# A delta rule stage that starts each chunk with the queries, and wide products beside a router's narrow ones

## The reference, cut to what matters

```python
# gated delta rule, one chunk (8 heads; the kernel's chunks have 128 tokens, four in all)
v_new = u_c - w_c @ state
out   = q_c @ state + qk_c @ v_new
state = state * gl_c + k_c.T @ v_new        # read by the next chunk only
# router
g_idx = top_1(softmax(t @ w_grp)); e_idx = top_2(softmax(in_group(t @ w_rt)))
# after the experts: two gathered rows per token are weighted and added,
# then a norm (with a layer norm ahead of it after the first mixture)
h = h + w1 * y[row1] + w2 * y[row2]
```

## Time and profile before

| | |
|---|---|
| median of 3 runs (range) | 2215.73 us (2214.52 to 2217.94) |
| the profiled execution's own time | 2216.83 us |
| its span, from first to last instruction | 2215.1 us |
| around the span | 1.7 us |
| mean granted TensorE clock in the span | 0.969 |

### The profile page before, as it was taken

How to read it: one execution, slowest core, us unless ns; L and a number is a source line. 1 busy time by engine, 2 the same in 40 slices (tenths; PEclk the granted TensorE clock), 3 DMA queues, 4 the chain that set the end, 5 groups by cost and what they waited for, 6 DMA issues and landing times. The chain is left out here.

```text
span 2215.1 us, 21061 instructions
## 1 busy us (share of the span) xinstructions
PE 2118.0 (96%) x8072; PEld 1209.1 (55%) x8072; DVE 907.8 (41%) x1686; ACT 509.3 (23%) x1116; POOL 140.0 (6%) x210
## 2 busy tenths in 40 slices
PE   8999999999999999999799999999998989999995
PEld 4444445488874445444345478454445568654442
DVE  2435446345453125113444666242234467433223
ACT  1111111034341001111331146110004446311000
POOL 1000000001001000100200000000001000001003
PEclk9999999999999998999899999989998999989997
DMA  5334575410022114899636920239993220046996
GB/s 178 91 85 124 156 248 204 145 28 1 2 95 73 71 67 160 301 390 380 240 117 215 336 74 1 69 117 373 387 385 118 81 77 1 3 152 234 371 367 241
DMA packets 206470, 374.25 MB, mean 169 GB/s; under 512 B 22952, under 2 KB 124568, under 8 KB 206112
## 3 DMA queue, kind: packets, MB, share of 16 engines
q1 hardware_dynamic: 87568, 174.13, 24.0%
q10 hardware_dynamic: 105696, 157.30, 20.0%
q0 software_dynamic: 13104, 41.43, 5.1%
HBM read 335.60 MB, written 43.52 MB: 171 GB/s over the span
## 5 line engine op out<-in xcount | busy, mean ns | idle before, releaser
L1543 PE MATMUL bank<-ring,work 128*128 128x512 f32 x768 | 338.4, 593 | 7.5 <-DVE work L1559 3.8
L1543 PEld LDWEIGHTS bank<-ring,work 128*128 128x128 f32 x768 | 142.1, 190 | 170.4 <-issue 165.7
L1554 PE MATMUL bank<-ring_halves,work 128*128 128x512 f32 x384 | 173.0, 593 | 4.0 <-DVE work L1568 4.0
L414 PE MATMUL bank<-featT,ring 128*128 128x512 f32 x384 | 170.8, 598 | 4.6 <-DMA ring<-in_w_in 4.6
L2266 PE MATMUL bank<-ring,featT 128*128 128x512 f32 x384 | 170.7, 606 | 4.2 <-ACT featT L1946 2.6
L1283 PE MATMUL bank<-ring,work 128*128 128x512 f32 x384 | 168.9, 600 | 2.9 <-PEq L2043 1.9
L1565 DVE TENSOR_TENSOR work<-work,bank 128x256 f32<-128x256 f32 x48 | 20.2, 421 | 291.4 <-ACT work L1562 291.4
L2266 PEld LDWEIGHTS bank<-ring,featT 128*128 128x128 f32 x384 | 74.3, 195 | 96.5 <-issue 94.8
L1283 PEld LDWEIGHTS bank<-ring,work 128*128 128x128 f32 x384 | 73.2, 193 | 92.7 <-issue 92.7
L414 PEld LDWEIGHTS bank<-featT,ring 128*128 128x128 f32 x384 | 72.0, 192 | 86.8 <-issue 82.1
L513 PE MATMUL bank<-ring,featT 128*128 128x512 f32 x256 | 110.4, 593 | 0.9 <-PEq L396 0.9
(11 more groups left out here) (427 smaller groups left out, 2900.5 us busy)
## 6 DMA issues: line engine op xcount, KB each, us to landing
ring<-in_w_in SPq DMA_DIRECT2D x16, 2048.0 KB, 13.7
ring<-in_moe_w_gate ACTq DMA_DIRECT2D x28, 1024.0 KB, 9.2
ring<-in_moe_w_up ACTq DMA_DIRECT2D x28, 1024.0 KB, 11.7
ring_halves<-in_moe_w_down ACTq DMA_DIRECT2D x28, 1024.0 KB, 11.3
ring_halves<-in_w_ada SPq DMA_DIRECT2D x48, 512.0 KB, 6.3
y_rows<-work ACTq DMA_DIRECT2D x48, 512.0 KB, 10.8
ring<-in_expert_w_gate ACTq DMA_DIRECT2D x14, 1024.0 KB, 10.3
ring<-in_expert_w_up ACTq DMA_DIRECT2D x14, 1024.0 KB, 13.1
```

Source lines behind the costliest of these rows:

```text
L414: last = nc.tensor.matmul(bank[b % 4][:, :], w[:, k, (b % 4) * P:(b % 4 + 1) * P], featT[:, k, :], start=(k == 0), stop=(k == KD - 1))
L1543: last = nc.tensor.matmul(bank[2 + par][:, :], xgT[par][:, k, :], w_gu[par][:, k, :], start=(k == 0), stop=(k == KD - 1))
L1554: last = nc.tensor.matmul(bank[5 + h][:, :], hT[par][:, k, :], w_dn[par][:, k, span(h)], start=(k == 0), stop=(k == KF - 1))
```

## The change

The change has three parts. In the delta stage each chunk starts with `qT`; ACT copies it ahead of `g`, `e`. The eight `z` products of a chunk stand in four places (`Z_AT`): two at the chunk's start, four behind `kT` (six in the first chunk), one behind the last level, one behind `vn`. The banks of `o` and `s` change so that `sums` wait for `("o", 1)` and only `kT` for `("s", 1)`; DVE does both `oq`, both `sg`, both `o`, both `s`; the last chunk has no state update. In the routers `keep_clock(1)` stands between the logits, `turn(3)` comes before `logits(2)`, `ranks` are followed by two instead of one, `slots` by four instead of five. In the combines DVE's and ACT's copies come ahead of statistics and of the next root, the second `add` of tile 1 comes behind the copies in `cb_b`, and `keep_clock` products are added around the first turn.

```diff
-        pe_n = (["sums", "qT", "kT", "z"] + [("kk", u) for u in units] + ...
+        pe_n = (["qT", "sums", "kT"] + [("kk", u) for u in units] + ...
-        ac_n = (["g", "e", ("qT", 0), ("qT", 1), "rest", "decay", "z"] + ...
+        ac_n = ([("qT", 0), ("qT", 1), "g", "e", "rest", "decay"] + ...
...
-        QS_BANK, O_BANK, S_BANK, Z_BANK = (5, 6), (4, 0), (1, 2), 7
+        Z_AT = (2, 6, 7)
+        QS_BANK, O_BANK, S_BANK, Z_BANK = (5, 6), (0, 1), (5, 6), 7
...
                     if c:
                         AC.wait(pe, "z", c - 1)
-                        z_products(c, 0, KD // 2)
-                        DV.wait(pe, ("s", 1), c - 1)
+                        z_products(c, 0, Z_AT[0])
+                    (transposes of the queries, "qT")
+                    if c:
+                        DV.wait(pe, ("o", 1), c - 1)
                     (running sums, "sums")
-                    (transposes of the queries, "qT")
+                    if c:
+                        DV.wait(pe, ("s", 1), c - 1)
                     (transposes of the keys, "kT")
-                    PE.done(z_products(c, KD // 2 if c else 0, KD), "z")
+                    z_products(c, Z_AT[0] if c else 0, Z_AT[1])
...
+                    z_products(c, Z_AT[1], Z_AT[2])
                     DV.wait(pe, ("add", NL - 1, units[-1]), c)
...
+                    PE.done(z_products(c, Z_AT[2], KD), "z")
                     AC.wait(pe, ("vn", 1), c)
...
-                    for h in halves:
+                    for h in halves if c < T - 1 else ():
+                        DV.wait(pe, ("oq", h), c)
                         (state update, ("s", h))
...
                     logits(0)
+                    keep_clock(1)
                     logits(1)
+                    if gain is None:
+                        keep_clock(1)
+                    turn(3)
+                    keep_clock(1)
                     logits(2)
-                    turn(3)
                     PE.done(logits(3), "logits")
-                    DV.wait(pe, ("x", T - 1))
                     keep_clock(4)
...
-                    keep_clock(1)
+                    keep_clock(2)
...
-                    keep_clock(5)
+                    keep_clock(4)
...
+            def keep_clock(self, pe, n):
+                pe.wait_ge(AC.sem, AC.value(("row", 3)))
+                for _ in range(n):
+                    nc.tensor.matmul(bank[2][:, :], ident[:, :], level_mask[:, 0:4, :].rearrange("p a n -> p (a n)"), start=True, stop=True)
...
                 cb_a.sums(pe)
+                cb_a.keep_clock(pe, 2)
...
                 cb_a.turn(pe, 0, turn_banks)
+                cb_a.keep_clock(pe, 1)
                 job(0)
...
                 cb_a.norm(act, 0)
+                cb_a.keep_act(act, 0, turn_banks[0])
                 cb_a.ln_root(act, 1)
-                cb_a.keep_act(act, 0, turn_banks[0])
...
                 cb_a.add(dve, 1)
                 cb_a.keep_dve(dve, 0, turn_banks[1])
+                cb_a.statistics(dve, 1)
                 cb_a.layer_norm(dve, 1)
...
                 cb_b.turn(pe, 0, turn_banks)
+                cb_b.keep_clock(pe, 2)
                 latent(0, 0)
...
-                cb_b.add(dve, 1)
+                cb_b.add(dve, 1, of=(0,))
                 cb_b.keep_dve(dve, 0, turn_banks[1])
+                cb_b.add(dve, 1, of=(1,))
                 cb_b.add(dve, 2)
```

More of the change, by code:

```diff
@@ L872, in _ @@
                 for c in range(T):
+                    PE.wait(act, "qT", c)
+                    for h in halves:
+                        AC.done(nc.scalar.activation(qT[:, hs(h), :], b4(3 + h), ACT.Copy), ("qT", h))
                     PE.wait(act, "sums", c)
@@ L876, in _ @@
                     AC.done(nc.scalar.activation(sc[:, 464:480], sc[:, 448:464], ACT.Exp), "e")
-                    PE.wait(act, "qT", c)
-                    for h in halves:
-                        AC.done(nc.scalar.activation(qT[:, hs(h), :], b4(3 + h), ACT.Copy), ("qT", h))
                     DV.wait(act, "rest", c)
@@ L901, in _ @@
                         AC.done(nc.scalar.activation(vnew[:, hs(h), :], b4(2 + h), ACT.Copy), ("vn", h))
+                    PE.wait(act, "z", c)
+                    AC.done(nc.scalar.activation(q_tok[:, c, 0:BANK], bank[Z_BANK][:, :], ACT.Copy), "z")
             @block.vector
@@ L1869, in add_names, with stat_names @@
             def add_names(self, t):
-                return [("add", t, 0), ("add", t, 1)] + ([("half", t, 0), ("half", t, 1), ("mean", t)] if self.ln else [])
+                return [("add", t, 0), ("add", t, 1)]
+            def stat_names(self, t):
+                return [("half", t, 0), ("half", t, 1), ("mean", t)]
             def ln_names(self, t):
@@ L1969, in add @@
                     dve.wait_ge(AC.sem, AC.value(("alpha", t)))
-                for i, w in enumerate((self.rows.w1, self.rows.w2)):
+                for i in of:
+                    w = (self.rows.w1, self.rows.w2)[i]
                     if i:
@@ L1974, in add, with statistics @@
                     DV.done(nc.vector.scalar_tensor_tensor(out=x, in0=self.rows.y_in[2 * t + i], scalar=w[:, t:t + 1], in1=x, op0=ALU.mult, op1=ALU.add), ("add", t, i))
-                if self.ln:
-                    dve.wait_ge(DV.sem, DV.value(("add", t, 1)))
-                    for h in range(2):
-                        DV.done(nc.vector.bn_stats(self.stats[t][:, 6 * h:6 * h + 6], resid[:, t, span(h)]), ("half", t, h))
-                    dve.wait_ge(DV.sem, DV.value(("half", t, 1)))
-                    DV.done(nc.vector.bn_aggr(self.mv[:, t, :], self.stats[t].rearrange("p (a b) -> p a b", a=2)), ("mean", t))
+            def statistics(self, dve, t):
+                dve.wait_ge(DV.sem, DV.value(("add", t, 1)))
+                for h in range(2):
+                    DV.done(nc.vector.bn_stats(self.stats[t][:, 6 * h:6 * h + 6], resid[:, t, span(h)]), ("half", t, h))
+                dve.wait_ge(DV.sem, DV.value(("half", t, 1)))
+                DV.done(nc.vector.bn_aggr(self.mv[:, t, :], self.stats[t].rearrange("p (a b) -> p a b", a=2)), ("mean", t))
             def layer_norm(self, dve, t):
@@ L2335, in _ @@
                 cb_a.add(dve, 0)
+                cb_a.statistics(dve, 0)
                 cb_a.layer_norm(dve, 0)
@@ L2344, in _ @@
                 cb_a.add(dve, 3)
+                cb_a.statistics(dve, 3)
                 cb_a.layer_norm(dve, 3)
```

39 lines of the change are left out of this document (23 added, 16 removed).

## The result

Over five runs each, the changed kernel takes 2195.74 us at the median (2194.21 to 2203.72) where before took 2216.0 us: 20.3 us less, a ratio of 0.9914 with a 95% interval of 0.9895 to 0.9934 (by the ratio the gain is 19.1 us, between 14.6 and 23.3). The forecast was 2202.3 us, in a range of 2192 to 2211. So sign and range held, and the size was 6.6 us too small. The profiled execution took 2195.26 us with a span of 2193.5; against that of before (2216.83) it is 21.6 us shorter.

A forecast was written before the change was run, and what follows sets the result against it. TensorE was taken as the bound (records cover 96% of the span), losing time to waits and half clock. Delta stage 9.6, routers 0 and combines 3.8 made 13.4 off 2216.83: 2203.4, so 2202.3 us at the median; range 2192 to 2211.

The forecast's parts named there:

- The two holes of the delta stage: Delta stage: TensorE's waits before ks and o, each covered by one z product; 6.2 us gained over 4 chunks.
- The new stall: Delta stage: POOL's product ahead of DVE's clip delays kk by 0.9 in chunks 1 to 3; 2.7 us lost.
- POOL and DVE don't take turns: Rival, delta stage: the two engines do not block each other, so 2.7 less, 2199.6 us; chance 0.07.
- The end: Delta stage: from the last o group to the next stage 3.1 us instead of 7.43, saving 4.3.
- The clock at the next stage's head: Stage after the delta stage: shorter stillness may remove its half-clock start; worth up to 1.7 us, taken as 1.5.
- `o`, `s`, and DVE's eight steps behind them: Delta stage's end: the work said to fill the 7.43 us before the next stage, cut to 3.1.
- Held ones, late ones, early ones and the idle before the gather about cancel: I take 0: Routers: net gain taken as 0, with bounds of 12.6 us gained and 12 + 5 lost.
- The held case: Rival, routers: wide products hold the clock, ranks 13.8 and 14.6 after first logits; 2190 to 2194 us; chance 0.20.
- up to 1.7: Routers: if the clock falls in the wait for the gather, each first expert loses this; times 3 = 5 us.
- routers fell early: Rival, routers: the clock falls early and added products double in price; costs 5 to 12, 2207 to 2214 us; chance 0.18.
- 1.1 at once: First combine: the projection's wait of 2.61 shrinks to about 1.5 as only copies remain; 1.1 us gained.
- 1.5 for the clock: First combine: added products remove part of the 3.1 us half-clock cost of the projection's 16 records; 1.5 taken.

The follow-up runs named there:

- e4: Changed kernel with GpSimd's key product made to wait for VectorE's clip; 2199.6 us, median of 10 runs, ratio to before 0.9933.
- e7: Changed kernel with the last chunk's state update kept, as before had it; one run, delta stage 206.78 us, no total given.
- e2: Before with the routers' edits alone; 2212.17 us, median of 12 runs, ratio 0.9995 (0.9978 to 1.0011).
- e5: Changed kernel with six wide products behind slots in place of four; 2195.9 us, median of 6 runs, ratio to before 0.9909.
- e6: Changed kernel with GpSimd's key product behind the clip and six wide products behind slots; 2188.33 us, median of 6 runs, ratio 0.9895.
- e3: Before with the combines' edits alone; 2207.67 us, median of 12 runs, ratio 0.9972 (0.9957 to 0.9987).
- e9: Changed kernel run again unedited, on another call's chip; 2193.71 us, median of 6 runs, ratio to before 0.9918.
- e1: Before with the delta stage's edits alone; 2204.29 us, median of 12 runs, ratio 0.9958 (0.9941 to 0.9975).
- e10: Changed kernel with key product behind the clip, six products behind slots, and a wide product between third and fourth logits; 2194.14 us, ratio to before 0.9911.

## Why the prediction was right, and where it was too small

**Confirmed as written.** The two holes of the delta stage: no idle before `ks`, 0.1 left at `o` (0.19 was allowed). The new stall: POOL ahead of the clip, the clip 1.61 long (1.6), `kk` 0.69 idle from the modelled end, about 0.8 by the starts, in chunks 1 to 3 and not in chunk 0; e4 prices it at 2.76 in all where 2.7 was worked out, so the rival "POOL and DVE don't take turns" is out. The end: 3.09 from the last `o` (3.1), with the later load hidden. The clock at the next stage's head: 1.70 (1.5). The whole stage with that head measured 10.4 where 9.6 was forecast.

**Right in size, wrong in cause.** "`o`, `s`, and DVE's eight steps behind them" gave the end rightly, and 4.34 was measured for 4.3 (the steps behind the last `o` are seven, since the first `oq` stood ahead of it); but the sum did not part it. Most of it (2.55) stays with the update kept (e7), and so does the clock's 1.7. The rows of DVE put that part down to the regrouping of its steps, of which the prediction asked only whether it costs something.

**The routers: the step that failed** is "Held ones, late ones, early ones and the idle before the gather about cancel: I take 0". The held case was worked out to a few hundredths (13.8 and 14.6 forecast, 13.71 and 14.62 measured where it held), but was given 0.20 of the chance. In the changed kernel it is the common case: routers 2 and 3 held in each of the five traces with these edits, router 1 in two of them, and it fell late in the other three, two of them 2.8 us behind the held case and one 1.1 (1.2 to 2.9 forecast). The argument against it, that logits 2 and 3 make 3.6 us of narrow work and before fell after 2.7, did not carry: 3.65 passed at the full clock. The other half of the balance was there and larger than priced: the heads gave back 5.7 us in the mean of the five traces, up to 3.1 in one head, where "up to 1.7" each was allowed. Had both been priced at what the traces show, the term would have been +3.8, and the forecast 2198.5. That the total of e2 is near the 0 forecast is partly luck: the held case was underrated and so was its price in the heads. That routers fell early in the other direction is seen in one router of e5 and e6, not in a trace of the changed kernel.

**The combines: a mis-sized term.** 3.8 was forecast; e3 gives 6.2 by its ratio (2.9 to 9.5), and the distances 3.8 for the first combine (mean 14.1 to mean 10.2) and 1.5 for the second (10.2 to 8.7; to 8.0 if all nine kernels with both edits are taken). The second was forecast at 1.2, and the profiled pair has 1.18: a start 1.0 later and a job 2.2 shorter. The first was "1.1 at once" and 1.5 for the clock. The start moved by 1.93 (4.55 to 2.62 from the first turn to the job). Of this 1.05 is the 1.1; the turn itself had been at half clock and became 0.9 shorter, which the sum left out. The job became 1.7 to 2.5 shorter.

**The sum.** Delta 10.4, routers 3.8, combines 5.3 to 6.2 make 19.5 to 20.4, beside 20.3 by the medians, 19.1 by the ratio, and 18.2 by the ratio of e9. The totals of e1, e2 and e3 alone add up to 9.3 + 1.1 + 6.2 = 16.6, uncertain by some 6, so they neither show nor exclude that the parts help one another. The profiled pair differs by 21.6, since its routers gained 5.8. By the estimate from spans and granted clocks, e9 loses 44.6 us to the half clock and before in the same call 62.6, so 18.0 of the 18.9 by which their means differ; the rest of the time is 7.9 us shorter than before's in e1, but 9.6 and 2.3 longer in e2 and e3, so the added products take about what the removed waits gave.

**What stays open.** Why the clock falls in router 1 in some executions and holds in others at the same program, why it fell in router 3 of both e5 and e6 and of no trace of the changed kernel, and why the second combine's first turn is at the full clock in e4, e6 and e10 and in no other kernel with both edits. No experiment here tells what sets it. Whether e6 or e10 is faster than the changed kernel in total is not settled: what each of their edits does in its own stage is.

## What to carry to other kernels

Filling a stretch with wide products to hold TensorE's clock only moves the question to the next wait. Follow the clock there and price that too: here waits of 1.99 us and more for the gather cost 1.4 to 3.1 us each, and two products in front of them kept what the routers' products had won. When an instruction leaves the chain ahead of GpSimd, look at what it then starts beside on VectorE; one added wait gave back 2.76 us. And before crediting a gain at a stage's end to the work that was deleted, count which engine's steps are the last there: here more than half of it was there with that work kept.

## What the runs showed of the hardware

A fall of the clock comes at few prices in stretches with full work. The stage behind the delta stage took 29.2 or 27.5 us to its first transposes, and stretches that no edit touches also came in lengths 1.6 to 1.7 apart: 177.75 or 179.44 from there to router 1, and 61.2, 62.8 or once 64.5 from the first combine's last turn to the first products behind its projection. The heads that fell cost 1.4 to 1.75 where the granted clock was low for 3.4 us, and 2.9 to 3.1 where it was low for 6.8. Windows of e6, and then of e5, over the same place of one of them, where TensorE stands still for 1.05 us in both, at the start of the projection ahead of router 1:

```profile
788.00:800.00 12.00, 11.68 (x24) 5.10 (x25) 1.38 (x2) 1.28 (x1) 2.66 (x16) 0.86 0.66 219
```

```profile
790.00:802.00 12.00, 11.27 (x27) 5.08 (x28) 1.80 (x3) 1.28 (x1) 2.66 (x16) 1.00 0.69 231
```

The granted clock is 0.86 in one and 1.00 in the other, and 0.14 of 12 us is the 1.7 by which the stretches differ. Such places lie all along the program, and most of the spread of single runs goes with them: over the 33 runs of before, the time and the estimate of what is lost to the half clock (span times one minus mean granted clock) have a correlation of 0.88. An edit of 2 or 3 us is seen in distances within its trace long before it is seen in its total.
